# Three moves of weight loads and placements around the second layer's state-space mixer, on one core

## What is computed

```python
def swiglu(h, w_gate, w_up, w_down):                      # layer 0, second half
    return (jax.nn.silu(h @ w_gate) * (h @ w_up)) @ w_down

def s5_mixer(h, w_in, ...):                               # layer 1, first half
    u = (h @ w_in).astype(f32).reshape(bsz, t, S5_GROUPS, S5_GROUP)
    ...
    _, _, x_re, x_im = lax.associative_scan(combine, (a_re_t, a_im_t, bu_re, bu_im), axis=1)
    y = (jnp.einsum('gip,btgp->btgi', c_re, x_re) - jnp.einsum('gip,btgp->btgi', c_im, x_im)
         + d_skip.astype(f32) * u).reshape(bsz, t, S5_WIDTH)

for layer in range(DEPTH):
    mod = (cs @ w_ada[layer] + b_ada[layer])[:, None, :]
    sh_m, sc_m, gt_m, sh_f, sc_f, gt_f = jnp.split(mod, 6, axis=-1)
    h = rmsnorm(x, g_norm[layer, 0]) * (1 + sc_m) + sh_m
    ...
    x = x + gt_m * rmsnorm(o, g_norm[layer, 1])
```

## Time and profile before

| | us |
|---|---|
| median of 3 runs (1841.28 to 1846.24) | 1842.84 |
| the profiled execution | 1847.72 |
| its span in the profile | 1845.9 |
| TensorE busy in the span | 1734.2 (94%) |
| VectorE, ScalarE busy | 1379.5, 1201.8 |

### The profile page before, as it was taken

One profiled execution on the slowest core, in us unless ns is written; L12 is line 12 of the kernel. 1 busy time (PEld: TensorE's weight loads), 2 busy tenths in 40 slices (PEclk: granted clock), 3 DMA queues, 4 the chain that ended last, 5 costly groups with the idle time before them and its releaser, 6 DMA issues.

```text
span 1845.9 us, 27103 instructions
## 1 busy us (share of the span) xinstructions
PE 1734.2 (94%) x9191; PEld 1457.0 (79%) x9191; DVE 1379.5 (75%) x1579; ACT 1201.8 (65%) x1491; POOL 146.4 (8%) x199
## 2 busy tenths in 40 slices
PE   6988899998899797999999999999999999999994
PEld 3877799986779695887887878878878788788884
DVE  3564445491643736998998989989989899899997
ACT  3623355303463445878888888888888888888885
POOL 1041000000044300700000000000000000000001
PEclk8988999999865698999999999999999999999997
DMA  8662654335630249998998989989989899899995
GB/s 349 257 258 90 237 194 160 141 151 194 289 137 1 103 178 382 399 418 323 422 367 348 410 312 419 392 325 420 360 358 400 314 422 380 343 412 355 399 376 197
DMA packets 72903, 553.49 MB, mean 300 GB/s; under 512 B 8256, under 2 KB 8527, under 8 KB 15328
## 3 DMA queue, kind: packets, MB, share of 16 engines
q1 hardware_dynamic: 69186, 538.54, 73.9%
q0 software_dynamic: 3072, 12.54, 1.8%
q10 hardware_dynamic: 542, 1.20, 0.2%
HBM read 530.74 MB, written 21.53 MB: 299 GB/s over the span
## 4 chain that ended last, share of the span: by engine, by line
PE 84%; DVE 6%; issue 4%; DMA 3%; ACT 2%; POOL 1%; ACTq 0%; DVEq 0%; POOLq 0%; SPq 0%
PE bank L1939 81%; PE bank L2406 1%; DMA ring<-in_dense_rows_dram 1%; DVE w_lo L516 1%; DMA arena<-in_state_conv_dram 1%; DVE arena L1686 1%; ACT w_hi L511 1%; DVE sq L1364 0%; PE bank L2385 0%; DVE rstd L1346 0%; ACT w_hi L463 0%; DVE w_lo L469 0%; DMA fT<-y_rows,row_i 0%; DVE sq L1517 0%; DVE arena L1899 0%
## 5 line engine op out<-in xcount | busy, mean ns | idle before, releaser
L1939 PE MATMUL bank<-w_hi,parts 128*128 128x512 f32 x3024 | 899.0, 392 | 14.8 <-DVE w_lo L516 13.3
L516 DVE TENSOR_TENSOR w_lo<-ring,w_hi 128x1024 fp32r<-128x1024 f32 x654 | 782.4, 1221 | 81.1 <-PE bank L1939 29.8
L511 ACT ACTIVATE w_hi<-ring 128x1024 fp32r<-128x1024 f32 x654 | 690.7, 1062 | 157.4 <-PE bank L1939 157.3
L1939 PEld LDWEIGHTS bank<-w_hi,parts 128*128 128x128 f32 x3024 | 561.6, 188 | 134.1 <-DVE w_lo L516 18.6
L1939 PE MATMUL bank<-w_lo,parts 128*128 128x512 f32 x1512 | 548.3, 390 | 0.0
L1939 PE MATMUL bank<-parts,w_hi 128*128 128x264 f32 x1600 | 312.6, 297 | 21.9 <-DVE parts L1353 21.9
L1939 PEld LDWEIGHTS bank<-w_lo,parts 128*128 128x128 f32 x1512 | 283.9, 188 | 60.3
L1939 PEld LDWEIGHTS bank<-parts,w_hi 128*128 128x128 f32 x1600 | 260.6, 198 | 33.9 <-issue 21.5
L1939 PE MATMUL bank<-parts,w_lo 128*128 128x264 f32 x800 | 234.0, 293 | 0.0
L469 DVE TENSOR_TENSOR w_lo<-ring,w_hi 128x2048 fp32r<-128x2048 f32 x50 | 114.5, 2295 | 148.2 <-ACT w_hi L463 148.2
L1939 PEld LDWEIGHTS bank<-parts,w_lo 128*128 128x128 f32 x800 | 158.0, 198 | 0.0
(11 more groups left out here) (412 smaller groups left out, 1289.4 us busy)
## 6 DMA issues: line engine op xcount, KB each, us to landing
ring<-in_expert_rows_dram SPq DMA_DIRECT2D x330, 1024.0 KB, 7.2
ring<-in_dense_rows_dram SPq DMA_DIRECT2D x48, 2048.0 KB, 8.3
hT<-in_expert_rows_dram SPq DMA_DIRECT2D x55, 1024.0 KB, 7.2
ring<-in_dense_rows_dram SPq DMA_DIRECT2D x8, 1408.0 KB, 6.4
x_rows<-arena SPq DMA_DIRECT2D x1, 7168.0 KB, 28.8
y_rows<-arena SPq DMA_DIRECT2D x10, 512.0 KB, 6.6
arena<-x_rows SPq DMA_DIRECT2D x9, 512.0 KB, 8.1
ring<-in_dense_rows_dram SPq DMA_DIRECT2D x2, 1024.0 KB, 4.8
```

The source lines that it names most:

```text
L511: act.activation(hi_slots[u % AHEAD], raw_unit(u), ACT.Copy).then_inc(hi_ready, 1)
L516: dve.tensor_tensor(lo_slots[u % AHEAD], raw_unit(u), hi_slots[u % AHEAD].bitcast(F32), ALU.subtract).then_inc(lo_ready, 1)
L1939: return pe.matmul(out, lhsT, rhs, start=start, stop=stop, skip_group_check=True)
```

## The change

The first piece of a down pair gets a semaphore of its own, `down_first`, which TensorE raises behind the pair's first half, and `used` names it for the first pieces. In `PIECES`, ada 14 to 16 and in1's second piece change places: in1's second piece comes straight behind pair 3's, then ada 14 to 21. On TensorE and ScalarE ada 16 leaves its place before in1; rounds 0 to 3 hold ada 16 to 19, rounds 1 to 4 their rows. On VectorE the two blocks of tiles 4 to 7 go into rounds 1 and 2, behind the rotation.

```diff
-SEQ += [("ada", _i) for _i in (14, 15, 16)] + [("in1", _t) for _t in range(KT)] + [("ada", _i) for _i in range(17, 22)]
+SEQ += [("ada", _i) for _i in (14, 15)] + [("in1", _t) for _t in range(KT)] + [("ada", _i) for _i in range(16, 22)]
...
     PIECES.append((("w_ffn_down", 0, 256 * (_i // 2), _i % 2 * FF // 2), FT // 2, 256))
-PIECES += [_ada_piece(i) for i in (14, 15, 16)]
 DENSE_PIECES.append((len(PIECES), "in1", 4))
 PIECES.append((("w_in1", 0, W), KT, W))
-PIECES += [_ada_piece(i) for i in range(17, 22)]
+PIECES += [_ada_piece(i) for i in range(14, 22)]
...
         for i in range(8):
-            used[DOWN_PIECES[i]] = (acc_full, TILES["down"] + 2 * (i // 2) + 2)
+            used[DOWN_PIECES[i]] = (acc_full, TILES["down"] + i + 1) if i % 2 else (down_first, i // 2 + 1)
...
@@ vector
-            for half in range(2):
-                dve.wait_ge(acc_free, TILES["in1"] + 4 * half + 4)
...
-            mod_rows(16)
+            def place_rows(ks, r):
...
+            dve.wait_ge(acc_free, TILES["in1"] + 4)
+            for r in range(4):
+                rows_placed = place_rows(slice(0, 4), r)
+            rows_placed.then_inc(u_first, 1)
...
                 if k:
                     scans(k - 1)
                     rotate_im(k - 1)
-                if 1 <= k <= 3:
-                    mod_rows(16 + k)
+                if 1 <= k <= 2:
+                    dve.wait_ge(acc_free, TILES["in1"] + KT)
+                    rows_placed = place_rows(slice(4, 8), k - 1)
+                    if k == 2:
+                        rows_placed.then_inc(u_second, 1)
+                if 1 <= k <= 4:
+                    mod_rows(15 + k)
...
@@ tensor
                         if half == 1:
                             ins.then_inc(acc_full, 1)
+                    if half == 0:
+                        ins.then_inc(down_first, 1)
...
-            ada(16)
-            dense(2, "in1")
-            ada_rows(16)
-            dense(KT - 2, first=2)
+            dense(KT, "in1")
...
-                if 1 <= k <= 3:
-                    ada_rows(16 + k)
-                if k < 3:
-                    ada(17 + k)
+                if 1 <= k <= 4:
+                    ada_rows(15 + k)
+                if k < 4:
+                    ada(16 + k)
```

More of the change, by code:

```diff
@@ L65 @@
 TILES = {name: TILE_AT[(name, 0)] for name in ("out0", "ffn", "down", "in1", "glu")}
-TILES["ada1b"] = TILE_AT[("ada", 17)]
+TILES["ada1b"] = TILE_AT[("ada", 16)]
 GROUPS = [range(i, min(i + 4, FT)) for i in range(0, FT, 4)]
@@ L394, in hybrid_trunk @@
             sem(n) for n in ("outs_t", "outs_copied_act", "outs_copied_dve", "y_stored"))
-        hid_ready, out_done = sem("hid_ready"), sem("out_done")
+        hid_ready, out_done, down_first = sem("hid_ready"), sem("out_done"), sem("down_first")
         pieces, at = [], 0
@@ L1680, in _ @@
             dve.wait_ge(u_cleared, 1)
-            for half in range(2):
-                dve.wait_ge(acc_free, TILES["in1"] + 4 * half + 4)
[L1683 to L1690, removed]
-            mod_rows(16)
+            def place_rows(ks, r):
+                for s_ in range(4):
+                    dve.tensor_copy(*place(ks, r, s_))
+                for at, s_ in ((0, 0), (CHUNKS + NS, 3)):
+                    ins = dve.tensor_copy(u_in[QUAD * s_:QUAD * s_ + QUAD, ks, r, at:at + NS],
+                                          uT[QUAD * r:QUAD * r + QUAD, ks, TP:T])
+                return ins
+            dve.wait_ge(acc_free, TILES["in1"] + 4)
+            for r in range(4):
+                rows_placed = place_rows(slice(0, 4), r)
+            rows_placed.then_inc(u_first, 1)
             def turn_back(k):
```

## The result

The changed kernel takes 1828.24 us (median of 4 runs, 1825.79 to 1831.0), the kernel before 1844.54 us beside it: ratio 0.9913, 95% interval [0.9896, 0.9929]. The profiled execution after took 1825.79 us, with a span of 1824.0 us.

The account below looks back on a forecast made before the run. TensorE, holding 84% of the chain, was taken to bound the kernel. Terms -6.1 - 2.6 - 0.8 - 0.3 + 0.5 + 0.8 = -8.5 us took the 1842.84 us median to 1834.3 us, range 1831.5 to 1841.0.

Parts of the forecast that it names:

- The down pairs: Fourth down pair: earlier release of its first piece removes the ring wait, -6.1 us, and the low clock, -2.6 us.
- Pair 3's end to in1: Between the last down pair and in1: removing ada 16 only lengthens a wait on VectorE's chain; 0, bound +1.0 us.
- Inside in1: In in1: the four small products that turn ada 16's row go, -0.8 us.
- VectorE's placements: Two blocks of copies move from before the rounds into rounds 1 and 2, saving TensorE's wait there, -0.3 us.
- The start of the rounds: Behind in1's end: another start can lose 1.0 us of full clock; 0 to +1.0, taken as +0.5 us.
- the rounds: Rounds 3 and 4 gain an ada piece and its row, partly repaid by full clock; +0.8 us, ends -0.6 and +4.7.
- Rival 3: In the rounds: full clock behind the ada pieces is lost, +8.8 us, 1851.6 us; chance 0.04.
- the prediction's own signs of being wrong: A wait at pair 3 for either piece, VectorE releasing in rounds 1 to 3, or later rounds over 14.6 us apart.
- Rivals 1 and 2: Rounds take back half, 1838.7 us, chance 0.17; pair 3's first piece comes no earlier, 1843.0 us, chance 0.05.
- Rival 4: Later rounds: the clock stays up, four of them saving 4.2 us each, 1817.5 us; chance 0.03.

Follow-up runs that it names:

- e4: Changed kernel with VectorE's placements of tiles 4 to 7 put back before the rounds; 1835.24 us, ratio 0.9946.
- e6: Changed kernel with eight extra 128x512 products, result unused and nothing more loaded, at the end of each of rounds 4 to 7; 1815.69 us, ratio 0.9838.
- e7: Changed kernel with glu's first 2 MB ring piece loaded ten times more during rounds 4 to 7, no product added; 1852.73 us.
- e13: Kernel before with ada 17 on TensorE ahead of the second lag products in round 0; 1842.09 us, ratio 0.999.
- e17: Changed kernel with twelve 128x1 VectorE copies into an array nothing reads, placed where VectorE is idle; 1809.68 us, ratio 0.9812.
- e18: e6 with the same twelve small VectorE copies as e17; 1801.31 us, ratio 0.9775.
- e12: e6 with the ada pieces of rounds 0 to 3 and the extra products in halves of four, at two places of a round; 1827.68 us.
- e11: e4 with ada 16 on TensorE ahead of the second lag products; 1832.37 us.
- e10: Changed kernel with the two blocks of tiles 4 to 7 placed before the rounds too, and again in rounds 1 and 2; 1814.42 us.
- e14: Kernel before with twelve more VectorE copies, two blocks of tiles 0 to 3 placed a second time before the rounds; 1832.7 us.

## Why the prediction was wrong, step by step

- **The down pairs**, -6.1 and -2.6: right. No ring wait, 19.74 us for pair 3. S1 differs by 11.1 us in the first pair of profiles and 8.2 in the second; some 2 us of such a difference arise before the change's place (ada 13 started at 362.40 after and 364.63 before in the first pair). Counted from there the two differences are 8.9 and 8.7.
- **Pair 3's end to in1**, 0 with a bound of +1.0: -0.9. Ada 15's wait stayed, as said; ada 15 and the mean squares behind it took 3.18 and 4.22 us for 3.64 and 4.74, the clock coming back sooner.
- **Inside in1**, -0.8: right, S3 is 0.9 us shorter.
- **VectorE's placements**, -0.3: mis-sized. The 0.27 us of the earlier trace rows was read as the whole wait; it is what was left of 1.04 us at half clock. With the other parts in place the move is worth 8.9 us in S4 (e4 against after) and some 7 in the medians (1835.2 and 1828.2).
- **The start of the rounds**, +0.5, and **the rounds**, +0.8: these failed. The prediction let another start only lose full clock ("0 to +1.0"), and gave each piece the stretch that it had had. In the profiles full clock lasted 8.9 us behind in1's end for some 5 before, the stretch behind the first piece 13.7 us for 3.9, and S4 came out 12.0 us shorter in place of 1.0 longer. (the earlier trace rows show 0.96 up to 511.5: by that the fall itself was at about 511.0, 5.1 us behind in1's end and not 5.6.) e6 and e7 show one half of the mechanism: wide products raise the clock among the small ones. The profile of e13 fits it for the kernel before: there the first wide product came 14.0 us behind in1's end, with the clock down for 8.4 us already. After the change it comes 9.9 us behind, less than 1 us after the fall, and full clock was back after 3.4 us for 13.7 us. What decides how long the clock stays up behind in1 was not found.
- **How far each part makes this** can't be told apart: S4 fell by 6.7, 4.8 and 6.9 us with one part each, 3.1 with two, 12.0 with all, each but the last from one profile. The clock's stretches are not a sum over edits. Rival 3 had this mechanism with the other sign only; that was the missing case. None of the prediction's own signs of being wrong appeared, and it named none for more full clock in rounds 0 to 2.
- **Rivals 1 and 2** fell: the clock answered the new piece (542.60), and no wait is left at pair 3. **Rival 4** fell: the later rounds are at 0.50 and 14.6 us apart (553.84, 568.45, 583.04 in the timeline). Its rule, from the Trainium skill, page "TensorE: Matmul & The Clock Gate", section "What's actually happening", that activity releases the clock, had been set against 25.00 busy us of 25.00 at 0.50. e6 bears the rule out for wide products only: in these rounds busy time with the small products alone went with 0.50, and eight wide ones a round brought 1.00.
- **Open**: over two profiles each, S1 to S5 fall by 22.5 us, the medians by 16.3. S6, with nothing changed in it and 60 packets in both, lies between 1151.8 and 1161.8 in single profiles and can hide some of this. The other part may lie in the profiled executions of the kernel before (1847.72 and 1850.29 us, above their kernel's medians). Their granted clock is 0.943 and 0.944, the median of their kernel 0.946, while the two after have their kernel's median, 0.951. The difference of 0.0025 is 4.6 us of 1845. If that lies in the rounds, a typical execution gained some 7 us there rather than 12. The medians fit this: without the rounds the stages fall by 9.7 us (S1 counted from ada 13), which leaves 6.6 of the 16.3. These are estimates; no trace of a typical execution of the kernel before was taken.

## What to carry to other kernels

Where TensorE is bound at half clock among small products, look for wide ones that can stand between them, and try it: even products whose result nobody uses paid here (-12.9 us in e6, -8.4 from e17 to e18), but the same products in halves lost the gain (e12), and placing one earlier did not pay reliably (e11, e13). A wait that is read in a stretch at half clock is only what that stretch has left of it; ask what it would be at full clock before pricing its removal. Before a stage of one profile is compared with that of another, see where the profiled executions stand among all of their kernel, in time and in granted clock. Compare variants by stage, and count the instruction packets of each: a gain in a stage that the edit doesn't touch may be the code's position.

## What the hardware showed that was not expected

Twelve VectorE instructions more, at three different places ahead of the mixture's loop, made the last stage some 20 us shorter in six of six kernels (e10, e14 to e18), with 25 packets on q14 in place of 60 or 61 in all others. The 35 packets that go are five for each of the loop's seven passes: in the trace of after they lie from 832.6 to 1676.7 us, in groups 121 us apart, and in e17 q14 has none between 822.0 and 1659.1. Of the time, 14 us of the 20 show as TensorE's idle time ahead of the mixture's products (15.6 us, then 1.5). The Trainium skill, page "Runtime: NRT & Kernel Launch", section "Instruction fetch mechanics", says that a taken branch to code outside the part that is held makes a fetch before execution goes on; the packets agree. How far the code may be moved before the gain is lost was not tried.

The rounds repeated to 0.1 us in two profiles of a kernel (130.30 and 130.24, 118.26 and 118.29). Yet the same program, up to the end of round 3, lost 6.9 us there in a third profile (e7), in which the clock fell 3.8 us sooner. In all executions of the kernel before, the time falls as the granted clock rises (correlation -0.74 over 81 of them).
